# Operand sums of the gates: fourteen of sixteen made by VectorE, two kept by POOL

## What is computed

```python
z = h @ w_in                       # 1024 -> 8*512 + 4*1024 columns
a_u, b_h, b_b, b_c, c_uv, d_in, g_in = jnp.split(z, SPLIT_POINTS, axis=-1)
...
sc_ext = jnp.concatenate([sconv_prev, b_c * b_h], axis=1)
b_out = b_b * causal_dwconv(sc_ext, sconv_w)                    # branch B
d_out = jax.nn.silu(layernorm(d_c, cconv_ln_g, cconv_ln_b))     # branch D
...
proj = jnp.einsum('blkw,kwd->blkd', branches, w_branch)
gates = jax.nn.sigmoid(g_in.reshape(Bn, L, N_BRANCH, D_MODEL) + b_gate)
merged = jnp.sum(gates * proj, axis=2)
```

## Time and profile before

| | |
|---|---|
| median of 3 runs | 2231.78 us (2228.2 to 2231.83) |
| profiled execution | 2232.29 us, of which the span of the engines 2230.5 |
| busy | TensorE 2143.1 us, weight loads 2078.6, VectorE 1386.0, ScalarE 682.0, POOL 879.2 |
| mean granted TensorE clock | 0.990 |
| chain that ended last | TensorE 85%, VectorE 9%, ScalarE 2% |
| waits of TensorE, 395 to 620 us | 7.2 us for VectorE L2878; 5.2 us in two for POOL's lo parts; 2.2 us for ScalarE's copy |

### The profile page before, as it was taken

The page is one execution under the profiler, slowest core; times in us unless marked ns, Lnnn a source line. Parts: engine busy times, 40 slices in busy tenths (PEclk is TensorE's granted clock), DMA queues, the critical chain, the costliest instruction groups (busy, mean ns, idle before and its releaser), DMA issues.

```text
span 2230.5 us, 35732 instructions
## 1 busy us (share of the span) xinstructions
PE 2143.1 (96%) x14656; PEld 2078.6 (93%) x14656; DVE 1386.0 (62%) x1609; ACT 682.0 (31%) x1091; POOL 879.2 (39%) x625
## 2 busy tenths in 40 slices
...
GB/s 213 147 81 85 109 136 80 59 49 84 105 97 118 93 104 199 137 200 155 158 46 39 111 16 167 132 90 61 158 149 153 119 148 289 241 149 156 120 72 81
DMA packets 230096, 273.58 MB, mean 123 GB/s; under 512 B 9656, under 2 KB 182712, under 8 KB 227879
## 3 DMA queue, kind: packets, MB, share of 16 engines
...
q0 software_dynamic: 256, 0.01, 0.0%
...
## 4 chain that ended last, share of the span: by engine, by line
PE 85%; DVE 9%; ACT 2%; issue 2%; DMA 1%; POOL 0%; ACTq 0%; DVEq 0%; SPq 0%; POOLq 0%
PE PS L1294 34%; PE PS L1574 15%; PE PS L1821 14%; PE PS L1766 14%; PE PS L1714 1%; PE PS L1676 1%; DVE slots_d L2596 1%; PE PS L1647 1%; DVE opnd L3162 1%; PE PS L1363 1%; PE PS L1325 1%; DVE w_lo L2619 1%; PE PS L1689 1%; PE PS L1632 0%; DMA opnd<-hid_scratch 0%
## 5 line engine op out<-in xcount | busy, mean ns | idle before, releaser
L1766 PE MATMUL PS<-opnd,slot 128*128 128x272 f32 x2688 | 341.2, 289 | 5.1 <-DVE opnd L3162 2.0
L1766 PEld LDWEIGHTS PS<-opnd,slot 128*128 128x128 f32 x2688 | 339.5, 189 | 6.6 <-issue 3.1
L1821 PE MATMUL PS<-opnd,slot 128*128 128x272 f32 x2640 | 336.0, 289 | 5.6 <-DVE opnd L3162 4.4
L1821 PEld LDWEIGHTS PS<-opnd,slot 128*128 128x128 f32 x2640 | 334.2, 189 | 6.3 <-DVE opnd L3162 4.9
L1109 POOL TENSOR_TENSOR slot<-raw_A,slot 128x512 fp32r<-128x512 f32 x160 | 239.9, 1506 | 242.4 <-ACT slot L1851 242.0
L1066 POOL TENSOR_TENSOR w_hi<-w_raw,ones 128x512 fp32r<-128x512 f32 x86 | 107.9, 1254 | 320.3 <-PE PS L1294 226.4
L1574 PE MATMUL PS<-g_opnd,g_slot 128*128 128x272 f32 x1536 | 198.0, 290 | 5.0 <-POOL g_slot L1109 5.0
L1574 PEld LDWEIGHTS PS<-g_opnd,g_slot 128*128 128x128 f32 x1536 | 196.1, 190 | 5.2 <-POOL g_slot L1109 5.2
L1294 PE MATMUL PS<-h_hi,w_hi 128*128 128x364 f32 x744 | 169.0, 336 | 13.4 <-DVE slots_d L2878 7.2
L1294 PE MATMUL PS<-h_lo,w_hi 128*128 128x364 f32 x744 | 165.5, 331 | 0.0
L1294 PE MATMUL PS<-h_hi,w_lo 128*128 128x364 f32 x744 | 165.5, 331 | 0.0
...
## 6 DMA issues: line engine op xcount, KB each, us to landing
...
```

Of the source, the lines that this page charges most:

```text
L1766: mm = mmul(product_of(u, p)[:, c, :], w, x[:, HC * c:HC * c + HC], start=(j == 0 and e == 0), stop=(j == PAIRS - 1 and e == 2))
L1821: mm = mmul(product2_of(t)[:, c, :], w, x[:, part, HC * c:HC * c + HC], start=(j == 0 and e == 0), stop=(j == 2 * PAIRS - 1 and e == 2))
```

## The change

VectorE takes over `gate_t12` for all four j, the lo parts of products 5 and 6, and `gate_t4` for j = 0 and 3. POOL keeps `gate_t4` for j = 1 and 2, which now start when the lo parts of product 6 for these j are there, and the lo parts of the weights. Two tables give the order in which hi and lo parts are counted. Shapes and the number of operations on each operand stay as they are.

```diff
+MADE = [(5, 0), (6, 0), (5, 1), (6, 1), (5, 2), (6, 2), (5, 3), (6, 3), (7, 0), (7, 1), (7, 2), (7, 3), (4, 0), (4, 3)]
+MADE_POOL = [(4, 1), (4, 2)]
+HI_OF = MADE[:8] + MADE_POOL + MADE[8:]
+LO_OF = ([(6, 1), (6, 2), (6, 0), (6, 3)] + [(5, j) for j in range(4)] + [(7, j) for j in range(4)]
+         + [(4, 1), (4, 2), (4, 0), (4, 3)])
```

POOL's list after the sample products of branch D:

```diff
-        pool.wait_ge(dn_sum, 1)
-        for j in range(PAIRS):
-            gate_t12(j)
-        for j in range(PAIRS):
-            gate_t12_lo(j)
-        for j in range(PAIRS - 1):
-            gate_t4(j)
-        for p in (1, 6, 2, 3):
-            gate_lo(0, p)
-        gate_t4(PAIRS - 1)
-        gate_lo(0, 5)
-        gate_lo(0, 7)
-        gate_lo(0, 4)
+        for j in (1, 2):
+            pool.wait_ge(g_op_lo, LO_OF.index((6, j)) + 1)
...
+        for p in ORDER_IN:
+            gate_lo(0, p)
```

ScalarE's list in block ct of the B stage:

```diff
             if ct == 3:
                 branch_d(2)
                 branch_d(3)
+                gate_operand_hi(4, 1)
+                gate_operand_hi(4, 2)
             if ct == 2:
-                for j in range(PAIRS):
-                    for p in (5, 6):
-                        gate_operand_hi(p, j)
+                for j in range(PAIRS - 1):
+                    gate_operand_hi(5, j)
+                    gate_operand_hi(6, j)
...
                 nc.scalar.activation(tmp[2][:, :], tmp[2][:, :], ACT.Sqrt).then_inc(dn_std, 1)
+                gate_operand_hi(5, PAIRS - 1)
+                gate_operand_hi(6, PAIRS - 1)
```

ScalarE's list in unit 0:

```diff
         gate_operand_hi(7, 0)
+        for p in (1, 6, 2):
+            gate_hi(0, p)
         gate_operand_hi(7, 1)
-        for p in (1, 6, 2, 3):
-            gate_hi(0, p)
         gate_operand_hi(7, 2)
+        gate_hi(0, 3)
+        gate_hi(0, 5)
+        store_ring(RING_B[3], br_dram[1, 3], ring_full, CT)
         gate_operand_hi(7, 3)
-        gate_hi(0, 5)
         gate_p1_copied(0)
-        store_ring(RING_B[3], br_dram[1, 3], ring_full, CT)
-        for j in range(PAIRS):
-            gate_operand_hi(4, j)
         gate_hi(0, 7)
         gate_hi(0, 4)
+        gate_operand_hi(4, 0)
+        gate_operand_hi(4, 3)
```

VectorE's list in block ct of the B stage:

```diff
+            if ct == 2:
+                gate_t12(2)
             wait_ready(n_c)
...
                 dve.sem_inc(dn_var, 1)
+                gate_t12(3)
+                gate_operand_lo(6, 1)
+                gate_operand_lo(6, 2)
             if ct == 3:
                 gate_sum(0, 7)
                 gate_sum(0, 6)
+                gate_sum(0, 3)
+                gate_t3(1)
...
             if ct == 2:
+                gate_operand_lo(6, 0)
+                gate_operand_lo(6, 3)
                 slab_lo(S_B + 3 * ct + 5)
+                for j in range(PAIRS):
+                    gate_operand_lo(5, j)
                 gate_t3(0)
-                gate_t3(1)
...
+            if ct == 1:
+                gate_t12(0)
+                gate_t12(1)
```

VectorE's list in unit 0:

```diff
-        gate_sum(0, 3)
+        gate_sum(0, 5)
         gate_t3(2)
         gate_t3(3)
-        gate_sum(0, 5)
-        gate_operand_lo(7, 0)
-        gate_operand_lo(7, 1)
+        gate_t4(0)
         gate_p6(0)
-        gate_operand_lo(7, 2)
-        gate_operand_lo(7, 3)
-        gate_operand_lo(4, 0)
+        gate_t4(3)
+        gate_p2(0)
+        for j in range(PAIRS):
+            gate_operand_lo(7, j)
         gate_operand_lo(4, 1)
-        gate_p2(0)
+        gate_operand_lo(4, 2)
+        gate_sum(1, 7)
...
         v.tensor_tensor(c12, gate_product(0, 3), two(u2), ALU.add).then_inc(g_taken, 1)
-        gate_operand_lo(4, 2)
+        gate_operand_lo(4, 0)
+        gate_operand_lo(4, 3)
+        gate_sum(1, 6)
...
         v.tensor_tensor(c12, gate_product(0, 5), c12, ALU.add)
-        gate_operand_lo(4, 3)
+        gate_sum(1, 3)
         gate_p7(0)
         v.tensor_tensor(c22, gate_product(0, 5), two(u3), ALU.add).then_inc(g_taken, 1)
-        for p in (7, 6, 3):
-            gate_sum(1, p)
```

More of the change, by code:

```diff
@@ L1117, in gate_lo @@
                 ALU.subtract).then_inc(g_w_lo, 1)
[L1119 to L1142, removed]
+        n = N_A_MAP[CT - 1]
+        pool.wait_ge(ready[n % 2], n // 2 + 1)
+        pool.wait_ge(state_out, 16 * (2 + 9 + 1 + 9))
+        for j in (1, 2):
+            pool.wait_ge(g_op_lo, LO_OF.index((6, j)) + 1)
             x = h_quarters(j)
@@ L2192, in _ @@
         store_rows("tail_b", tail_b, SCONV_H, SCONV_H, o["new_sconv_prompt"], o["new_sconv_sample"])
+        gate_hi(1, 6)
         gate_sigmoid(0, "12")
+        gate_hi(1, 7)
         gate_sigmoid(0, "22")
-        gate_hi(1, 6)
         gate_sigmoid(0, "21")
-        for p in (7, 5, 4, 2, 3):
+        for p in (5, 4, 2, 3):
             gate_hi(1, p)
```

45 lines of the change are left out of this document (30 added, 15 removed).

## The result

| | before | changed |
|---|---|---|
| median of the runs, us | 2231.81 (2228.2 to 2232.31, 4 runs) | 2214.03 (2212.39 to 2215.36, 4 runs) |
| ratio of the runs, 95% interval | | 0.9923 (0.9906 to 0.9941) |
| profiled execution, span, us | 2232.29, 2230.5 | 2213.22, 2211.5 |
| TensorE's waits, 395 to 620 us | 7.2 + 5.2 + 2.2 | 3.4 in two, and 0.3 |
| first gate unit, us | 32.60 | 26.88 |

The changed kernel is faster by 0.77% (0.59 to 0.94%). 2213.1 was forecast, 2209 to 2221 the range.

A forecast was written before the change was run, and what follows sets the result against it. TensorE, busy 2143.1 of 2230.5 us, was taken as the bound, losing 10.0 us in the B stage and 11.6 in the first gate unit. Gains 9.9 + 8.8 = 18.7 us gave a median of 2213.1, range 2209 to 2221.

The forecast's parts named there:

- Part 1: Block 1, B stage: with gate_t12 off POOL, TensorE's wait at 447 and low clock go; gain 9.9 us.
- Part 4: Block 3 and first gate unit: 11.6 us lost before, less a new wait and low clock; gain 8.8 us.
- Part 2: The 28 operations VectorE takes over before the gates fit its idle time, 0.63 or 0.72 us each; cost 0.
- The rival that the 1.78 us belonged to the operands: VectorE's slow sums come from h tiles TensorE streams, not POOL; 1.12 us more per operation, 2246 us; chance 0.04.
- Part 3: POOL's two groups of t4 run beside the drain and VectorE's reciprocal without slowing them; cost taken as 0.
- the open question: Whether VectorE's reciprocal takes turns with POOL's t4 sums: 0 taken, up to 5.4 us possible.
- new wait of about 2.0 us before product 4: First gate unit: VectorE's lo part for product 4 ready at 542.4, wanted at 540.5; bounds 0 and 4.5 us.
- 0.8 for the clock: First gate unit: time lost at the low clock after the new wait, half of the earlier 1.6 us.
- its sign, about 24 us: Sign that the forecast is right: the first gate unit takes about 24 us.
- the 3 us that would have spoken against the forecast: Sign of a wrong forecast: a TensorE wait over 3 us before products 3, 5, 7 or 4.
- The rival of whole turns of 1.29: VectorE pays 1.29 us per POOL operation between 515 and 543; 2218.9 us; chance 0.22, shared with a contending reciprocal.
- VectorE the bound: Slower rival: each of 34 operations VectorE takes costs 1.12 us more, against 5 us spare room; 2246 us; chance 0.04.

The follow-up runs named there:

- e2: Changed kernel with the 20 sums gate_t12 put back on POOL from dn_sum on and off VectorE's list; 2225.26 us.
- e4: Changed kernel with VectorE making gate_t4 for j = 1 and 2 too, POOL none; 2217.44 us.
- e10: e5 with VectorE's t4(3) moved into its idle time ahead of block 3; 2211.08 us, changed kernel in the same runs 2215.40.
- e9: Changed kernel with four extra POOL operations in the first gate unit (lo part of product 7 made twice, of product 4 four times); 2216.47 us.
- e5: Changed kernel with VectorE's first gate unit reordered and its work ahead of the gates laid earlier, same operations; 2212.53 us.

## Why the prediction was right, point by point

**Time.** 2213.1 was forecast, 2214.0 measured, and 2214.8 and 2215.4 in later sets of runs: a gain of 16 to 18 us instead of 18.7. By the trace at the start of unit 1 the gain is 16.4 us (396.13 against 379.72 us from the reciprocal), 2.3 less than the sum; the scatter of a run is of the same size, so the first median looks closer than the working was. Part 1 won 0.8 more than forecast and part 4 won 3.1 less, and 2.0 us of the profiled execution's gain are scatter behind the change; that the first median came within 0.9 us is in part luck.

**Part 1**, forecast 9.9: right. 10.7 us to the gate's first product (363.53 against 352.84 from the reciprocal), of which 9.9 stand up to one and the same matmul behind the low clock (301.08 against 291.20, at 470.23 and 460.49) and 0.8 later, in block 2 and just ahead of the gates; e2 takes 9.2 back. L2880 begins when block 0's durations said, to 0.2 us (442.19; 442.0 was worked out).

**Part 2**, forecast 0: right. Every sum at 0.72 or 0.73 us, fifteen of the twenty in idle time; `t12(2)` ended at 469.0 with 2.7 us to spare where 2.6 was forecast. The rival that the 1.78 us belonged to the operands is gone: the same h tiles, TensorE busy, POOL idle, 0.72.

**Part 3**, forecast 0: right, and the open question is settled by two runs. 6.94 us with POOL beside, 6.95 in e4 without. The Trainium skill (SBUF — State Buffer, Who interferes with whom) names one SBUF input outside the 2-port modes as free of contention; the trace agrees for the reciprocal. L2868, which reads one tensor in SBUF and pays turns (last section), is not settled by this: whether it runs in a 2-port mode no run here shows.

**Part 4**, forecast 8.8: mis-sized, 5.7 won (32.60 to 26.88). Products 6 and 3 lost their waits as worked out, and the new wait stood where the forecast put it, before product 4. The step that failed is its size, "a **new wait of about 2.0 us before product 4**", with 0.8 for the clock. Clean, the unit takes 21.2 us (e10), 3.03 a product; against that the changed kernel loses, from start to start, 0.5 us up to product 5, 0.8 before product 7, 3.1 before product 4 and 1.3 at the low clock (4.36 less 3.03), together 5.7 instead of 2.8. So the unit missed its sign, about 24 us, and the wait stayed by 0.1 us under the 3 us that would have spoken against the forecast. Two terms of VectorE's list were too small. A turn was taken as 0.8 and is 0.96 by seven rows, 0.98 by e9. And `t3(1)`, taken to fit in before the ring product, met two turns and ended at 522.6: 2 us of turns stood there, and the ring product came 1.1 us late. The wait before product 7 I did not see, though its lo parts stand in the same list. ScalarE's copy of product 1 ended at 531.1, 0.2 us ahead of product 3 and not 1.3. The rival of whole turns of 1.29 is further from the measured 0.96 than the 0.8 taken was, and so is its time, 2218.9.

**VectorE the bound**, the slower rival, had its mechanism wrong (part 2), but VectorE's list does set one place: from 509 us to product 4 its list has no room (e4, e9), but the room ahead of 509 was there (e2, e5), so the sign never was in danger.
